# One-core decoder block: banks of the gather, order of early loads, waits and the final branch

## The reference

```
h = rmsnorm(x); P = h @ w_in                      # q, k/v, gates, retention q/k/v/g, merge gates
y_a = nsa_attention(...); y_r = retention(...)
x = x + (sigmoid(gate_a) * (y_a @ w_nsa_up) + sigmoid(gate_r) * (y_r @ w_ret_up)) @ w_out
h = rmsnorm(x)
group = argmax(h @ w_rg + b); two experts of the group = top_k(h @ w_re + b, 2)
x = x + sum over the two of  c_e * ((silu(h @ w_gate[e]) * (h @ w_up[e])) @ w_down[e])
out = rmsnorm(x)
```

## Time and profile before

| | before |
|---|---|
| median of 3 runs (lowest to highest) | 481.65 us (481.51 to 481.92) |
| profiled execution, its own time | 481.76 us |
| its span, first to last instruction | 480.0 us |
| TensorE matmul busy / weight loads busy | 440.5 us (92%) / 232.3 us (48%) |
| TensorE busy in 40 slices of 12 us, in tenths | 8999999999999999999999989999995867958962 |
| VectorE, ScalarE, GpSimd busy | 190.9 us, 79.2 us, 23.0 us |
| DMA | 150.76 MB, mean 314 GB/s |

### The profile page before, as it was taken

One profiled execution on the slowest core, in us unless ns is written; L12 is line 12 of the kernel. 1 busy time (PEld: TensorE's weight loads), 2 busy tenths in 40 slices (PEclk: granted clock), 3 DMA queues, 4 the chain that ended last, 5 costly groups with the idle time before them and its releaser, 6 DMA issues.

```text
span 480.0 us, 5788 instructions
## 1 busy us (share of the span) xinstructions
PE 440.5 (92%) x2278; PEld 232.3 (48%) x2278; DVE 190.9 (40%) x431; ACT 79.2 (16%) x214; POOL 23.0 (5%) x43
## 2 busy tenths in 40 slices
PE   8999999999999999999999989999995867958962
PEld 5599744555555555454444775355351411514321
DVE  1563037827954758778831243021020100201013
ACT  1000131423153011110002351011010100101112
POOL 2020000310000010100002110000000000000000
PEclk9999999999999999999999999999997995988998
DMA  8999648409308007959998599999999999999982
GB/s 256 430 421 363 212 147 320 207 1 382 144 0 348 3 0 281 397 197 436 398 359 339 188 352 392 417 434 427 418 432 431 421 433 417 433 431 424 425 356 93
DMA packets 25387, 150.76 MB, mean 314 GB/s; under 512 B 5484, under 2 KB 7949, under 8 KB 18446
## 3 DMA queue, kind: packets, MB, share of 16 engines
q1 hardware_dynamic: 19728, 146.83, 74.9%
q10 hardware_dynamic: 5630, 3.53, 2.3%
HBM read 147.73 MB, written 2.62 MB: 313 GB/s over the span
## 4 chain that ended last, share of the span: by engine, by line
PE 52%; issue 41%; DVE 3%; DMA 1%; SPq 1%; ACT 0%; POOLq 0%; POOL 0%; DVEq 0%; ACTq 0%
PE bank L721 31%; PE bank L696 19%; PE bank L727 2%; DMA ring<-in_dense 1%; DVE ring L1742 0%; DVE nsa L1651 0%; ACT hT_and_y L1625 0%; SPq L462 0%; SPq L464 0%; DVE ring L1748 0%; POOLq L150 0%; DVE qkT L1770 0%; DVE hT_and_y L1764 0%; DVE hT_and_y L1761 0%; DVE vr_and_gr L1884 0%
## 5 line engine op out<-in xcount | busy, mean ns | idle before, releaser
L721 PE MATMUL bank<-ring,x 128*128 128x512 f32 x128 | 57.3, 594 | 0.0
L696 PE MATMUL bank<-ring,nsa 128*32 128x512 f32 x304 | 41.8, 688 | 12.5 <-DMA ring<-in_moe_gate_up 12.4
L2136 DVE SCALAR_TENSOR_TENSOR wr<-cst,bank 128x256 f32<-128x256 f32 x8 | 3.4, 422 | 110.2 <-ACT cst L1581 110.2
L721 PE MATMUL bank<-ring,hT_and_y 128*128 128x512 f32 x96 | 43.4, 597 | 0.0
L721 PEld LDWEIGHTS bank<-ring,x 128*128 128x128 f32 x128 | 23.9, 190 | 27.6 <-issue 27.5
L1149 PEld LDWEIGHTS bank<-selection,Tb 128*128 128x128 f32 x256 | 30.6, 196 | 8.1 <-issue 8.1
L1149 PE MATMUL bank<-selection,Tb 128*128 128x128 f32 x256 | 32.9, 283 | 0.8 <-DVE selection L2058 0.8
L2127 DVE COPY nsa<-bank 128x512 f32<-128x512 f32 (+1 forms) x19 | 12.1, 635 | 48.3 <-PE bank L696 26.6
L696 PEld LDWEIGHTS bank<-ring,nsa 128*32 128x32 f32 x304 | 9.7, 118 | 42.2 <-issue 22.3
L696 PE MATMUL bank<-hT_and_y,ring 128*128 128x256 f32 x128 | 28.2, 380 | 0.1
L721 PEld LDWEIGHTS bank<-ring,hT_and_y 128*128 128x128 f32 x96 | 17.6, 190 | 20.1 <-issue 20.1
(11 more groups left out here) (259 smaller groups left out, 629.9 us busy)
## 6 DMA issues: line engine op xcount, KB each, us to landing
ring<-in_moe_gate_up SPq DMA_DIRECT2D x18, 2048.0 KB, 19.6
ring<-in_dense SPq DMA_DIRECT2D x17, 2048.0 KB, 9.7
spare<-in_moe_gate_up SPq DMA_DIRECT2D x4, 2048.0 KB, 23.7
hT_and_y<-in_moe_gate_up SPq DMA_DIRECT2D x4, 2048.0 KB, 25.6
vr_and_gr<-in_moe_gate_up SPq DMA_DIRECT2D x3, 2048.0 KB, 25.8
nsa<-in_moe_down SPq DMA_DIRECT2D x11, 512.0 KB, 17.0
windows<-in_moe_down SPq DMA_DIRECT2D x7, 512.0 KB, 15.7
qkT<-in_moe_down SPq DMA_DIRECT2D x7, 512.0 KB, 16.2
```

What stands on the lines that cost most here:

```text
L696: return nc.tensor.matmul(o, l, r, start=s, stop=e)
L721: ins = nc.tensor.matmul(o, l[:, k, :], r[:, k, :], start=first and k == 0, stop=last and k == n - 1, skip_group_check=True)
L2136: V.scalar_tensor_tensor(hid_e, th_sb, 1.0, bank[k][:, 0:FF], ALU.add, ALU.mult).then_inc(s_hch, 1)
```

## The change

Start: ScalarE issues the five parts of `qr`, and its small tables wait for the third part; the identity follows `xT` and `x` on the sync engine. TensorE's first scores wait for `qT0` alone of the two. `grZ` is done in two halves around `PcT`, and `attend(1)` comes after the first `grW` product. In the hand-over the router stream of a tile uses one tile's room of `h2T`, the down half of expert 10 is loaded behind `mT11`, that of expert 9 behind `out1`, and homes move accordingly. The first gather uses the banks of `G0`, `F0`, `G1`, in this order; the part of `G1` for tile 1 and `counts` stand behind the first gate-up piece (`gather_rest`). In the bodies `O0` is placed ahead of `G1` in the order of banks; TensorE's own order in the bodies stays. VectorE copies `G0` of the first gather. The branch after the first round is written with a hint, whose location is marked before the last segment.

```diff
@@ -104,7 +104,7 @@
-            ("pos0", 1), ("x2T11", 0), ("route1", 0), ("x2T12", 2), ("pos1", 1), ("F0", 2), ("counts", 2)]
+            ("pos0", 1), ("x2T11", 0), ("route1", 0), ("x2T12", 2), ("pos1", 2), ("counts", 2)]
@@ -122,9 +122,9 @@
-GATHER_N, DOWN_C, FINAL_C = ["G0.n", "G1.n"], ["O0.c", "O1.c"], ["NF0.c", "NF1.c"]
+FINAL_C = ["NF0.c", "NF1.c"]
...
-SEG = dict(first=GATHER_N, body=BATCH_C + GATHER_N + DOWN_C, last=FINAL_C + BATCH_C + [f"O{q}.c" for q in range(4)])
+SEG = dict(first=["G0.n", "F0.n", "G1.n"], body=BATCH_C + ["G0.n", "O0.c", "G1.n", "O1.c"], last=FINAL_C + BATCH_C + [f"O{q}.c" for q in range(4)])
@@ -279,10 +279,10 @@
-        o_sb = m0[:, 2048:3072].rearrange("p (h n) -> p h n", h=2)
+        o_sb = nsa[:, 3072:4096].rearrange("p (h n) -> p h n", h=2)
...
-        h2T = nsa[:, 0:2048].rearrange("p (k t) -> p k t", k=KT)
+        h2T = nsa[:, 0:1024].rearrange("p (k t) -> p k t", k=KT)
@@ -394,7 +394,7 @@
-        DW = [[b[:, 0:D] for b in down_homes] + [nsa[:, 3072:4096], m0[:, 1024:2048]], [b[:, D:2 * D] for b in down_homes] + [cst[:, C_ROT:C_ROT + D]]]
+        DW = [[b[:, 0:D] for b in down_homes] + [nsa[:, 2048:3072], m0[:, 1024:2048]], [b[:, D:2 * D] for b in down_homes] + [cst[:, C_ROT:C_ROT + D]]]
@@ -432,16 +432,20 @@
+            ahead = eng.mark_branch_hint_location()
...
-            return eng.value_load(nround_i[0:1, 0:1], min_val=1, max_val=ROUNDS)
...
-        def rounds(eng, body):
...
-            left = body(0)
-            with eng.If(left > 1):
+            return eng.value_load(nround_i[0:1, 0:1], min_val=1, max_val=ROUNDS), ahead
...
+        def rounds(eng, body, name):
...
+            left, ahead = body(0)
+            more, over = f"{name}_more_rounds", f"{name}_rounds_over"
+            eng.br_cond(left < 2, on_true=over, on_false=more).branch_hint(ahead)
+            with nc.body(more, valid_engines=[eng.engine]):
...
+            nc.switch_bb(over)
@@ -460,10 +464,7 @@
-                w = slice(ks[0] * 512, (ks[-1] + 1) * 512)
-                sp.dma_start(slot("qr")[:, w], dense("qr")[:, w]).then_inc(s_first[i], 16)
-                if i == 1:
-                    sp.dma_start(cst[:, 0:C_MC], a["packed"][:, 0:C_MC]).then_inc(s_cst, 16)
+            sp.dma_start(cst[:, 0:C_MC], a["packed"][:, 0:C_MC]).then_inc(s_cst, 16)
@@ -526,17 +527,19 @@
             first_gu(2)
             sp.wait_ge(s_mrg, 4)
             first_dw(1)
+            sp.wait_ge(*is_full("mT10"))
+            sp.wait_ge(*is_full("mT11"))
+            first_dw(10, (0,))
+            sp.wait_ge(*is_full("out1"))
+            first_dw(9, (0,))
             sp.wait_ge(*is_full("out2"))
             first_gu(4)
             sp.wait_ge(*is_full("out3"))
             gu_half(5, 0)
             sp.wait_ge(*is_full("out4"))
             gu_half(5, 1)
-            first_dw(9, (0,))
             sp.wait_ge(s_xr, len(PIECES))
             first_dw(9, (1,))
-            sp.wait_ge(*is_full("route1"))
-            first_dw(10, (0,))
             sp.wait_ge(s_seed, 4)
             first_dw(5)
 
@@ -801,7 +804,7 @@
-            have("qT0", "qT1", "ksT", "kwT")
+            have("qT0", "ksT", "kwT")
@@ -871,7 +874,7 @@
-            have("cmpkv")
+            have("cmpkv", "qT1")
@@ -893,15 +896,16 @@
-            done("grZ", product(oZ[:, :], h_sums[:, 0], b11))
+            product(oZ[:, :], h_sums[:, 0], b11, ks=range(2))
...
+            done("grZ", product(oZ[:, :], h_sums[:, 0], b11, ks=range(2, 4)))
...
-            attend(1)
...
+            attend(1)
@@ -1079,18 +1083,18 @@
-                    ins = mm(o[:, 0:NG + NE], h2T[:, k, t * P:(t + 1) * P], wr[:, k, :], k == 0, k == KT - 1)
+                    ins = mm(o[:, 0:NG + NE], h2T[:, k, :], wr[:, k, :], k == 0, k == KT - 1)
...
+                if t == 1:
+                    pe.wait_ge(s_member, 1)
+                    mm(o[:, 0:NE], ones[:, :], comb1[:, 0, :], True, False)
...
-                    ins = mm(o[:, 0:NE], tri, onehot[:, t, i, :], i == 0, i == 1 and t == 0)
-                if t == 1:
-                    pe.wait_ge(s_member, 1)
-                    ins = mm(o[:, 0:NE], ones[:, :], comb1[:, 0, :], False, True)
+                    ins = mm(o[:, 0:NE], tri, onehot[:, t, i, :], i == 0 and t == 0, i == 1)
@@ -1155,31 +1159,30 @@
-                        end(f"G{h}.n", ins)
+                        ins.then_inc(full[place("body", f"G{h}.n", 0)[0]], 1)
...
+                    g0 = start("G0.n")
+                    if isinstance(r, int):
+                        pe.wait_ge(s_xn, 1)
+                    pe.wait_ge(s_sel, n * TT + 1)
+                    gather_steps(0, g0, 2, 4)
+                    f0 = start("F0.n")
+                    gather_steps(0, f0, 0, 2)
+                    gather_part(n, 0, 1, start("G1.n"))
+                    if isinstance(r, int):
+                        places(1)
+                        pe.wait_ge(s_xn, 2)
+                    pe.wait_ge(s_sel, n * TT + 2)
+                    end("F0.n", gather_steps(1, f0, 0, 2))
+                    end("G0.n", gather_steps(1, g0, 2, 4))
...
-                        os = [start(f"G{h}.n") for h in range(2)]
-                        for t in range(TT):
-                            pe.wait_ge(s_sel, n * TT + t + 1)
-                            for h, o in enumerate(os):
-                                gather_part(n, t, h, o)
-                        return
-                    f0, g0 = begin("F0"), start("G0.n")
-                    pe.wait_ge(s_xn, 1)
-                    pe.wait_ge(s_sel, 1)
-                    gather_steps(0, f0, 0, 2)
-                    gather_steps(0, g0, 2, 4)
-                    g1 = start("G1.n")
-                    gather_part(n, 0, 1, g1)
-                    places(1)
-                    pe.wait_ge(s_xn, 2)
-                    pe.wait_ge(s_sel, 2)
-                    done("F0", gather_steps(1, f0, 0, 2))
-                    end("G0.n", gather_steps(1, g0, 2, 4))
-                    gather_part(n, 1, 1, g1)
-                    counts()
+                        out("F0.n")
+                        gather_rest(n)
...
+                def gather_rest(n):
+                    gather_part(n, 1, 1, bank[place("first", "G1.n", r)[0]])
@@ -1205,9 +1208,11 @@
-                            pe.wait_ge(*is_emptied("F0"))
+                            pe.wait_ge(*step_out("first", "F0.n", r))
...
-                            pe.wait_ge(*step_out("body", "G0.n", r, b - 1))
+                            gather_rest(n)
+                            counts()
+                            pe.wait_ge(*step_out("first", "G0.n", r))
@@ -1348,7 +1353,10 @@
-            act.wait_ge(s_xT[0], 16)
+            for i, ks in enumerate(FIRST):
+                w = slice(ks[0] * 512, (ks[-1] + 1) * 512)
+                act.dma_start(slot("qr")[:, w], dense("qr")[:, w]).then_inc(s_first[i], 16)
+            act.wait_ge(s_first[2], 16)
@@ -1523,7 +1531,9 @@
-                copy(j, h2T[:, k0:k1, t * P:(t + 1) * P], o[:, 0:(k1 - k0) * P].rearrange("p (k t) -> p k t", k=k1 - k0))
+                if t == 1:
+                    act.wait_ge(*is_full("route0"))
+                copy(j, h2T[:, k0:k1, :], o[:, 0:(k1 - k0) * P].rearrange("p (k t) -> p k t", k=k1 - k0))
@@ -1580,12 +1590,7 @@
-                    if isinstance(r, int):
-                        o = take("F0")
-                        copy("F0", hg[:, 0:2, :], o[:, 0:2 * P].rearrange("p (k s) -> p k s", k=2))
-                        out_of("G0.n", hg[:, 2:4, :].rearrange("p k s -> p (k s)"), slice(0, 2 * P))
-                        return
-                    gathered()
+                    out_of("F0.n", hg[:, 0:2, :].rearrange("p k s -> p (k s)"), slice(0, 2 * P))
@@ -2095,7 +2100,7 @@
-            def routing_weights():
+            def count_rounds():
@@ -2104,6 +2109,9 @@
+            def routing_weights():
@@ -2153,11 +2161,13 @@
-                        gathered()
-                        return
+                    out_of("G0.n", hg[:, 2:4, :].rearrange("p k s -> p (k s)"), slice(0, 2 * P))
+                    if isinstance(r, int):
+                        routing_weights()
...
-                    routing_weights()
-                    select_weights(n, 0)
+                    if isinstance(r, int):
+                        count_rounds()
+                        select_weights(n, 0)
@@ -1617,1 +1622,1 @@
-            rounds(act, one_round)
+            rounds(act, one_round, "scalar")
...
```

More of the change, by code:

```diff
@@ L597, in one_round @@
                             load_dw(h, j + BE, j, b * BE + BE)
-            rounds(sp, one_round)
+            rounds(sp, one_round, "sync")
             for h in range(TT):
@@ L1334, in one_round @@
                 steps("last", r, 0, weights(NB - 1))
-            rounds(pe, one_round)
+            rounds(pe, one_round, "tensor")
         @block.scalar
@@ L2189, in one_round @@
                 V.memset(st[:, 222:223], 0.0)
-            rounds(dve, one_round)
```

(1 more changed line is left out.)

## The result

The changed kernel took 478.22 us (median of 4 runs, 477.78 to 478.97), the kernel before 481.78 beside it (4 runs, 481.51 to 482.12): a ratio of 0.9925, 95% interval 0.9906 to 0.9944. That is 3.6 us faster, where 2.3 were forecast (479.35). The range of 477.7 to 481.7 holds it; the narrower one of the forecast itself, 478.6 to 480.3, doesn't. The profiled execution took 478.51 with a span of 476.6, so 3.4 us of span are to be found.

The account below looks back on a forecast made before the run. The prediction took TensorE to bound the first half and expert loads the second. Its terms, 0.2 + 0.73 - 0.3 + 1.65, summed to 2.3 us off 481.65, giving 479.35; range 477.7 to 481.7, the forecast's own 478.6 to 480.3.

Parts of the forecast that it names:

- A: Start: `qr` issued by ScalarE, small tables later; gain 0.2 us, bounds gain 0.7 and loss 1.5.
- B: First scores: they no longer wait for `qT1`; gain 0.73 us, bounds 0 and 0.73.
- C: Dense part: `grZ` split, `attend(1)` behind the first `grW` product, which waits for its bank; loss 0.3 us.
- D: Hand-over to the experts: early down halves, three-bank gather, earlier first reload; gain 1.65 us, bounds 0 and 2.3.
- everything arrives: Rival: in the dense part both stalls go, gaining 0.9 us instead of losing 0.3; 478.15 us, 17 in 100.
- edit (1): Hand-over: two down halves issued ahead of the DMA hole around 266 us, filling 2.4 us of it.
- (2): Hand-over: the gather uses three banks, so the first gate-up piece starts 1.65 us sooner.
- E: Expert bodies: `G1` waits 0.7 us for the copy of `HT.c` in each of 7, hidden by load waits; cost 0.
- rival of 484.25: Bodies: the wait of `G1` for `HT.c` decides, costing 4.9 us against gains of 2.3; 6 in 100.
- F: Branch after the first round, announced by a hint: engines branch while they wait; gain 0, bounds 0 and 0.2 us.
- The queue isn't empty: Rival: at the hand-over old loads last as long as the new reload, so nothing is gained there; 481.0 us, 10 in 100.
- late tables: Rival: at the start the small tables land late, a loss of 1.5 us; 481.05 us, 15 in 100.

Follow-up runs that it names:

- e9: The kernel before, unedited, profiled once more; a profile alone, with an output stage of 9.50 us.
- e1: The changed kernel run again with no edit: 478.05 us, ratio 0.9931.
- e8: The changed kernel with the bodies' bank order of before and `attend(1)` again ahead of the first `grW` product, `grZ` still split: 478.06 us.
- e6: The changed kernel with the old gather (tile 1's part of `G1` and `counts` ahead of the first piece), early down halves kept: median 1.83 us above e1.
- e5: The changed kernel with the two early down halves loaded late again, behind `out4` and `route1`: median 0.68 us above e1.
- e7: The changed kernel with both the late down halves and the old gather of before: median 0.85 us above e1.
- e4: The changed kernel with the bodies' bank order of before, so `G1` no longer takes the bank of `HT.c`: 478.01 us.
- e10: The changed kernel with the branch written as before, run a second time: 479.21 us.
- e11: The changed kernel with the start of before (`qr` issued by the sync engine, small tables ahead of all): 478.85 us.
- e12: The changed kernel with the dense order of before (first scores wait for `qT1`, `grZ` whole, `attend(1)` ahead of `grW`): 478.65 us.

## Why the prediction was right, and where it wasn't

Its direction, its range and most of its mechanisms held. The forecast of 2.3 us to the last sums met 2.30 in the first pair of profiles. That was luck: the terms erred both ways, and between the second profiles of the same two kernels (e9 and e1) it is 3.22. A term forecast at nothing, the branch, brought the rest, and put the measured time below the forecast's own range.

**A, forecast 0.2, measured 0.20 in the first pair and 0.8 over all profiles: mis-sized.** The step that failed was "it isn't short of issues, so most of that wait stays". The share of 1.00 at 4 to 6 us didn't mean that DMA had no room: with the new start it moved 290 GB/s there instead of 244, and at 6 to 8 us (before, then after):

```profile
6.00:8.00 2.00, 2.00 (x6) 0.90 (x5) 0.00 (x0) 0.17 (x1) 0.00 (x0) 1.00 0.87 257
```

```profile
6.00:8.00 2.00, 2.00 (x4) 0.73 (x3) 0.35 (x1) 0.00 (x0) 0.00 (x0) 1.00 1.04 416
```

The third and fifth parts of `qr` were issued at 3.53 and 7.42 us before; now all five are out by 3.36. With the old start the third pair of `qr` is waited for 0.95, 0.74, 0.38 and 0.15 us; with the new one no such row is left, though in five of the ten profiles a wait of 0.18 to 0.44 us stands ahead of the last four matmuls before R. "`R` begins near 18.3" was the slow end of what the new start gives. The tables' copy did begin at 15.58, right ahead of GpSimd's power at 16.03, where I had put it; R didn't wait for it.

**B, 0.73 forecast, and C, -0.3 forecast: 0.34 together where 0.43 was summed.** R to the first scores became shorter by 0.80 us (39.53 to 38.73), and the scores to the third gate product longer by 0.46. The mechanism of C, the order of the banks, was right (the wait is for VectorE L1807, which is L1802 of the earlier trace rows), and so was the size of the wait: TensorE resumed at 129.06, and with the 1.0 us gained before it that is 130.06 on the old time line, where 130.05 was forecast. The term left out is in "after it the same matmuls follow in either order": from there to the third gate product they took 6.73 us before (129.75 to 136.48) and 6.88 after (129.06 to 135.94). The rows say no more than that the same matmuls cost 0.15 us more in the new order. e8 shows the other order to be 0.47 better in all. The rival "everything arrives" had the right total by a wrong route: its gain of 0.9 in C didn't come.

**D, 1.65 forecast: right at its place, smaller at the end.** The first piece came 1.55 us sooner relative to the gather. "The wait for `G1`'s copy goes" is shown by e6, where it is back at 2.81. The ones product of `pos1` went ahead of the wait, "counted at nothing", and the stage from gate to gather became 0.27 us shorter (147.74 to 147.47). The rows ahead of the second gather, before and after, fit that edit; no run undoes it alone:

```profile
282.62 0.60 PE L696 MATMUL bank<-selection,cst 128*128 128x32 f32 x4 [0.34 <-DVE selection L2077]
283.06 0.39 PE L696 MATMUL bank<-member,ones 128*128 128x32 f32 x2
```

```profile
281.76 0.31 PE L699 MATMUL bank<-member,ones 128*128 128x32 f32 x2
282.01 0.63 PE L699 MATMUL bank<-selection,cst 128*128 128x32 f32 x4
```

From the start of the product with `selection`, which waits for VectorE, to the end of the last one it was 0.83 us before and is 0.63 now. "Without edit (1) they would eat the whole of (2)" is borne out in the main by e5 and e7: of 1.56 us the medians keep 0.17, the profiles 0.65. But that a microsecond gained at the reload is one at the end did not hold. From e7 to e1 the first piece moved by 1.80 us (1.57 by the gather, 0.23 by the start), and the end of the wait for the last piece by 1.18 (456.94 to 455.76), the last sums by 1.18 too, and the median by 0.85. Both waited for that piece equally long (0.77 and 0.76 us), so it is the loads that came only 1.18 sooner; where the other 0.6 went stays open. In the first pair this didn't show (2.37 at the reload, 2.30 at the sums).

**E, forecast at nothing: right.** The wait appeared with the forecast size (0.83 against 0.7) and e4 puts its price at none. One sign that I had named for a failure, that TensorE no longer waits at the last piece, did appear in the first profile. It depends on the execution: e1, the same kernel, waited 0.76 us. The part on the clock below shows what goes with it. The rival of 484.25 is excluded.

**F, forecast 0 with bounds 0 and 0.2, measured 1.1 in the first pair, 1.4 over all profiles: the term that was wrong.** The failed step is that nothing follows from "ScalarE and the sync engine branch while they wait". They did pass the branch in time, as the equal 3.7 us up to the first output issue show; the cost came behind it, in the issues and the landing. I looked for the branch's cost at the first instruction behind it, where only VectorE's 0.21 us shows, and not at the output's issue and landing. ScalarE's issue of 2.02 us, twice that of the sync engine for the same 2 transfers, stood in the profile of before.

**"The queue isn't empty" and "late tables"** are excluded: e5 is what the first would look like, and R came earlier. That the branch might not do what it says would by my words have changed nothing; it would have cost a third of the gain.

**The clock at the last piece.** What TensorE brings to the last piece is in part taken back there. Means over 456 to 462 us of the changed kernel, which did not wait for that piece, and of e4, which waited 1.39 us (columns as above, the clock third from the end):

```profile
456.00:462.00 6.00, 4.33 (x52) 1.75 (x48) 0.89 (x3) 1.04 (x3) 0.00 (x0) 1.00 1.01 410
```

```profile
456.00:462.00 6.00, 4.54 (x44) 1.92 (x36) 1.27 (x3) 1.15 (x3) 0.00 (x0) 0.72 1.03 417
```

In e4 the granted clock was partly at its lower level, 1.2 GHz, and eight down matmuls took 1.08 us instead of 0.61 to 0.64. So e4 began the transposes behind the last piece 1.68 us before the first profile after (458.13 and 459.81), and its last sums only 0.34 (468.06 and 468.40).

The wait alone doesn't decide this: the first profile of the kernel before waited 1.77 us there and kept the clock at 1.00. What parts all fourteen profiles is one gate-up piece of the batch before, near 433 us. These are the rows of the changed kernel and of e1, the same kernel:

```profile
433.44 3.31 PE L699 MATMUL bank<-spare,nsa 128*32 128x512 f32 x16 [2.99 <-DMA spare<-in_moe_gate_up]
```

```profile
432.54 1.92 PE L699 MATMUL bank<-spare,nsa 128*32 128x512 f32 x16 [1.53 <-DMA spare<-in_moe_gate_up]
```

In six profiles (the first of before, the first after, e5, e10, e11, e12) that piece was waited for 2.94 to 2.99 us and its sixteen matmuls took 2.72 to 3.60 us; these kept the clock at the last piece, and five of them didn't wait for it. In the other eight the wait was 1.26 to 1.64 us and the matmuls took 1.92 or 1.93; these waited 0.76 to 2.33 us for the last piece and lost clock behind it. So an execution lost time to the clock at the one place or at the other, and the same kernel did either. From the transposes to the last sums it took 8.59 to 8.80 us with the clock kept and no late down halves, 9.25 and 9.40 with late ones (before and e5), and 9.68 to 11.18 with the clock lost. What sets which of the two an execution does stays open.

## What to carry to other kernels

Where loads bound the second half, look at what is in the DMA queue at the moment when the time is won: with old bytes still there, little of 1.56 us was left. Move the old bytes out first, then the restart, and test the two as a pair. Expect the end to give less than the restart did, and look for the clock in the last stages before you explain a wait there by one execution. Price a branch at the transfers and issues behind it, not at the first instruction behind it, and lay the stretches you compare at a row that both traces have. Before you explain a median, look whether the runs fall into two groups. When two edits' prices are under the noise of whole runs, cut the traces into stages between rows that both kernels have: here that resolved 0.01 us where the times resolved one.

## What the runs showed of the hardware

- With the old form of the branch the last transfers of 1 MB ended 1.1 to 2.1 us later. ScalarE's output landed after 3.7 to 4.3 us in all four profiles instead of 2.8 to 3.0, its two issues took 2.02 to 2.11 us in two of them instead of 0.96 (the sync engine's 2.30 instead of 1.00 in one), and an instruction packet of queue q8 moved in the first microsecond behind the output issue in all four and in none of the ten others.
- A share of 1.00 of the DMA engines at 4 to 6 us stood beside 244 GB/s with the old start. With the loads of `qr` issued by ScalarE beside those of the sync engine, that stretch moved 290 GB/s and the next one 416 instead of 257.
- From 433 us on, TensorE's clock fell to its lower level in every profile at one of two places: behind a wait of 2.94 to 2.99 us near 433 us (six profiles, sixteen matmuls in 2.72 to 3.60 us instead of 1.92), or behind the last piece (eight profiles, eight matmuls in 1.08 us instead of 0.64).
- The start is the least repeatable part: the same instructions reached R at 17.37 to 18.34 us, while the next 266 us, up to the first piece, repeated to some 0.02 us between kernels with the same edits.
